# Experts begin after a first group of tiles has its queries; the other tiles' queries run between expert products; 64x64 blocks; a ring of 8 gather buffers

## The reference, cut to what matters

```
q      = h @ peer_wq                    # 1024 -> 2048: 8 heads x 2 halves x 128
s[j]   = q[j] @ keys[j % 2]             # 16 score rows of 128 keys per token
top16  = of each half; then top 16 of the 16 x 16 sums: expert numbers, gates
a      = gelu(h . u[expert])            # 8 heads x 16 = 128 experts per token
x     += g * sum(gate * a * v[expert])  # v, u: rows of 1024
```

## Time and profile before

| | us |
|---|---|
| median of 3 executions | 5278.08 (5275.77 to 5279.01) |
| the profiled execution | 5270.96 |
| its span, first to last instruction | 5269.2 |

### The profile page before, as it was taken

The page is one execution under the profiler, slowest core; times in us unless marked ns, Lnnn a source line. Parts: engine busy times, 40 slices in busy tenths (PEclk is TensorE's granted clock), DMA queues, the critical chain, the costliest instruction groups (busy, mean ns, idle before and its releaser), DMA issues.

```text
span 5269.2 us, 37538 instructions
## 1 busy us (share of the span) xinstructions
PE 4275.7 (81%) x11220; PEld 2065.7 (39%) x11220; DVE 3146.8 (60%) x8145; ACT 492.9 (9%) x1467; POOL 1498.5 (28%) x1376
## 2 busy tenths in 40 slices
PE   8999999987777777777777778999887777777777
PEld 1477635552323333232332225765442323233322
DVE  1052322348878788787886652523367878788665
ACT  1131110100000000000000001211100000000100
POOL 0000000004434444343444330000004444344443
PEclk9877698998898988988889997787798898988999
DMA  7100032349999999999999991011139999999998
GB/s 253 50 9 17 20 112 84 98 158 381 415 405 420 404 419 414 407 420 402 419 415 407 421 380 39 9 32 37 60 118 422 415 406 418 401 422 415 407 422 354
DMA packets 277772, 1489.70 MB, mean 283 GB/s; under 512 B 24152, under 2 KB 69848, under 8 KB 112704
## 3 DMA queue, kind: packets, MB, share of 16 engines
q0 software_dynamic: 185888, 1347.13, 62.1%
q1 hardware_dynamic: 66512, 114.85, 6.6%
q10 hardware_dynamic: 25168, 25.32, 1.4%
HBM read 1474.52 MB, written 12.68 MB: 282 GB/s over the span
## 4 chain that ended last, share of the span: by engine, by line
PE 44%; DMA 30%; DVE 13%; issue 10%; POOL 2%; ACT 1%; DVEq 0%; ACTq 0%; POOLq 0%; SPq 0%
DMA X<-in_uv_dram,hT 29%; PE ps L782 11%; PE ps L427 8%; PE ps L750 4%; PE ps L566 4%; PE ps L448 3%; PE ps L603 3%; POOL X L1518 2%; PE ps L578 2%; DVE hT L1407 1%; DVE X L1415 1%; PE ps L631 1%; DVE X L1349 1%; DVE X L1347 1%; DVE X L1350 1%
## 5 line engine op out<-in xcount | busy, mean ns | idle before, releaser
L782 PE MATMUL ps<-X,hT 128*128 128x512 f32 x5120 | 2468.0, 636 | 834.1 <-DVE hT L1407 833.1
L1518 POOL DMA_INDIRECT X<-in_uv_dram,hT x1280 | 1423.0, 1112 | 2387.6 <-PE ps L782 1628.4
L782 PEld LDWEIGHTS ps<-X,hT 128*128 128x128 f32 x5120 | 1007.1, 203 | 2294.5 <-issue 1239.9
L1415 DVE CUSTOM_DVE_ANT_0 X<-hT,X 128x1024 f32<-128x1024 f32 x1280 | 1541.6, 1224 | 608.8 <-DMA X<-in_uv_dram,hT 577.3
L1069 ACT ACTIVATE hT<-hT 128x2 f32<-128x2 f32 x640 | 130.1, 203 | 3068.2 <-DVE hT L1415 3068.1
L1407 DVE TENSOR_SCALAR hT<-ident,hT 128x128 f32<-128x128 f32 x1280 | 383.5, 344 | 1.5 <-ACT hT L1069 1.5
L427 PE MATMUL ps<-wring,hT 128*128 128x512 f32 (+2 forms) x736 | 308.4, 581 | 2.5 <-ACT yT L939 1.4
L750 PE MATMUL ps<-hT,wring 128*128 128x512 f32 x512 | 227.6, 598 | 2.2 <-ACT hT L860 2.2
L1488 POOL TENSOR_TENSOR X<-X 128x256 f32<-128x256 f32 x32 | 23.1, 724 | 702.4 <-DVE att L1202 692.6
L448 PE MATMUL ps<-wring,cT 128*2 128x512 f32 x384 | 181.7, 629 | 39.7 <-DMA wring<-in_ada_w_dram 19.1
L566 PE MATMUL ps<-X 64*128 64x256 f32 (+3 forms) x464 | 208.9, 597 | 3.7 <-ACT yT L939 1.4
(11 more groups left out here) (239 smaller groups left out, 2754.9 us busy)
## 6 DMA issues: line engine op xcount, KB each, us to landing
wring<-in_ada_w_dram SPq DMA_DIRECT2D x48, 1024.0 KB, 5.1
wring<-in_w_in_dram SPq DMA_DIRECT2D x24, 1024.0 KB, 5.2
X<-in_uv_dram,hT POOLq DMA_INDIRECT x1280
wring<-in_peer_wq_dram SPq DMA_DIRECT2D x16, 1024.0 KB, 5.6
wring<-in_w_out_dram SPq DMA_DIRECT2D x8, 1024.0 KB, 5.0
X<-scores SPq DMA_DIRECT2D x8, 1024.0 KB, 9.6
X<-mods ACTq DMA_DIRECT2D x12, 512.0 KB, 9.0
scores<-X ACTq DMA_DIRECT2D x16, 384.0 KB
```

What stands on the lines that cost most here:

```text
L782: m = pe.matmul(ps[:, h, :], dg[:, s % 8, :], uvr[:, s % UVRING, D + 512 * h:D + 512 * h + 512], start=(s == 0), stop=(s == SLOTS - 1))
L1415: m = v.tensor_tensor_reduce(uvr[:, s_ % UVRING, 0:D], xt, uvr[:, s_ % UVRING, 0:D], 1.0, 0.0, ALU.mult, ALU.add, adot[:, s_:s_ + 1])
L1518: g.indirect_dma_start(uvr[:, s % UVRING, :], None, a["uv"], bass.IndirectOffsetOnAxis(ap=istages[i % 2][:, s:s + 1], axis=0)).then_inc(S( ...
```

## The change

- **Groups.** `FIRST_GROUP = (CT, 1)`: layer 0's first group is the two context tiles, layer 1's its first tile; the rest is the other group (four and three tiles). Queries, scores and the choice of tile 0 are made for the first group alone; then experts begin. In the last tile of the first group (`with_rest`: tile 1 in layer 0, tile 0 in layer 1) TensorE runs the rest's queries between the expert products: 128 products of 512 (384) columns spread over 52 pairs, keys and scores two and five pairs after a query is done; VectorE picks the next tile's keys and pairs there straight from `stage`. `peer_wq` (8 MB) is loaded a second time in that tile, and the scores of the rest (bar its first tile) are stored there.
- **Indices** go out head by head: GpSimd may issue the first gathers after the first head.
- **64x64 blocks.** The diagonal is 64 columns wide (`ident2` holds two 64x64 identities one above the other). A slot's product is four products 64x64x512 instead of two 128x128x512; two slots make eight, ordered so that four different quarters of the array follow each other. The two halves of the tile's sum lie in four banks, and are added at the tile's end: ScalarE copies half of each to `xt` (2 activations), VectorE adds (2) and then multiplies.
- **`em` per pair**, not per slot; the diagonal ring has 16 places of 64 columns (before 8 of 128).
- **Ring of 8** gather buffers: `UVRING = 8`.
- **Modulation in column groups.** Each product has 32 stationary columns (two and thirty zeros), and four k-blocks go to the four 32-column groups of the array; a product with `pick` (2 columns) adds the four partial rows, another the bias. TensorE takes the halves one at a time. The last two chunks of layer 1 move from after the scores to between the norm transposes.

```diff
-MOD_BEFORE_FFN = ((7, 8), (9,), (), (), (), ())
+MOD_BEFORE_FFN = ((7, 8), (9,), (10,), (11,), (), ())
-UVRING = 11
+FIRST_GROUP = (CT, 1)
+REST_PAIRS = 52
+REST_GATES_AT = 59
+UVRING = 8
+DGRING = 16
+def query_done(j):
+    return next(q for q in range(REST_PAIRS) if KD * 2 * PH * (q + 1) // REST_PAIRS >= KD * (j + 1))
+def keys_at(j):
+    return query_done(j) + 2
+def scores_at(j):
+    return query_done(j) + 5
 # SyncE
-                for q in range(2):
-                    sp.wait_ge(S(f"sd{q}"), B(f"sd{q}", L) + 16 * PH)
-                for i in range(TILES - lo - 1):
-                    sp.wait_ge(S("istg"), B("istg", L) + 2 + PH * i)
-                    sp.dma_start(scn, scores_d[i + lo + 1]).then_inc(S("sl"), 16)
+                first, rest = groups(L)
+                load_scores(first, 1)
+                for c in range(4):
+                    send(L, a["peer_wq"][L], c * CH, "fq", 2 * PH + 4 * (c + 1), False)
+                load_scores(rest, 2 if len(first) > 1 else 1)
 # TensorE, modulation
-                        g = take(2)
-                        for k in range(KD):
-                            m = pe.matmul(ps[0:2, 6 + c % 2, :], cT[:, k, :], wsl(g, k, 0, CH), start=(k == 0), stop=False)
+                        for half in range(2):
+                            g = take(1)
+                            for j in range(GROUP_K):
+                                m = pe.matmul(ps[32 * j:32 * j + 32, 6 + c % 2, :], cT[:, half * GROUP_K + j, :], wring[:, g % WRING, j, :],
+                                              start=(half == 0), stop=(half == 1))
+                        if n_:
+                            gather_parts(chunks[n_ - 1])
 # TensorE, experts
-                    for s in range(SLOTS):
-                        pe.wait_ge(S("dg"), B("dg", L) + SLOTS * i + s + 1)
-                        for h in range(2):
-                            m = pe.matmul(ps[:, h, :], dg[:, s % 8, :], uvr[:, s % UVRING, D + 512 * h:D + 512 * h + 512],
-                                          start=(s == 0), stop=(s == SLOTS - 1))
+                    for q in range(SLOTS // BATCH):
+                        s = q * BATCH
+                        pe.wait_ge(S("dg"), B("dg", L) + SLOTS * i + s + 2)
+                        for h in range(2):
+                            v0 = uvr[:, s % UVRING, D + 512 * h:D + 512 * h + 512]
+                            v1 = uvr[:, (s + 1) % UVRING, D + 512 * h:D + 512 * h + 512]
+                            ends = dict(start=(s == 0), stop=(s == SLOTS - 2))
+                            pe.matmul(ps[0:HD, h, :], dg(slice(0, HD), s), v0[0:HD], **ends)
+                            pe.matmul(ps[HD:P, 2 + h, :], dg(slice(HD, P), s), v0[HD:P], **ends)
+                            pe.matmul(ps[HD:P, h, :], dg(slice(0, HD), s + 1), v1[0:HD], **ends)
+                            m = pe.matmul(ps[0:HD, 2 + h, :], dg(slice(HD, P), s + 1), v1[HD:P], **ends)
                         m.then_inc(S("em"), 1)
+                        if i == len(first) - 1:
+                            for j in range(2 * PH):
+                                if keys_at(j) == q:
+                                    key_scores(rest, 1, j)
+                            blocks = KD * 2 * PH
+                            for b in range(blocks * q // REST_PAIRS, min(blocks, blocks * (q + 1) // REST_PAIRS)):
+                                query(rest, 1, b // KD, b % KD)
 # ScalarE, end of a tile
+                    act.wait_ge(S("em"), B("em", L) + (SLOTS // BATCH) * (i + 1))
+                    nc.scalar.activation(x2[0:HD], ps[HD:P, 0:2, :], ACT.Copy)
+                    nc.scalar.activation(x2[HD:P], ps[0:HD, 2:4, :], ACT.Copy).then_inc(S("fold"), 1)
 # VectorE, end of a tile
-                    v.tensor_tensor(gj, ps[:, 0:2, :], gtab[:, s, :].rearrange("p (a b) -> p a b", b=512), ALU.mult).then_inc(S("xa"), 1)
+                    v.tensor_tensor(gj[0:HD], ps[0:HD, 0:2, :], x2[0:HD], ALU.add)
+                    link(v.tensor_tensor(gj[HD:P], ps[HD:P, 2:4, :], x2[HD:P], ALU.add))
+                    v.tensor_tensor(g4, g4, gtabs[s], ALU.mult).then_inc(S("xa"), 1)
 # GpSimd
-                            g.wait_ge(S("em"), B("em", L) + SLOTS * i + used + 1)
+                            g.wait_ge(S("em"), B("em", L) + SLOTS // BATCH * i + (used + SLOTS) // BATCH - SLOTS // BATCH + 1)
```

More of the change, by code:

```diff
@@ L180, in slot_uses, with groups @@
     return (SLOTS - 1 - r) // UVRING + 1
+def groups(layer):
+    tiles = list(range((0, CT)[layer], TILES))
+    return tiles[:FIRST_GROUP[layer]], tiles[FIRST_GROUP[layer]:]
+def query_done(j):
[4 more added lines that the diff above has]
+    return query_done(j) + 5
 def att_base(kind, layer):
@@ L776, in _, with query @@
-                pe.wait_ge(S("fse"), B("fse", L) + 2 * PH)
+                first, rest = groups(L)
+                wq = [None]
+                def query(group, n_, j, k):
+                    c0, N = group[0] * P, len(group) * P
+                    if k == 0:
+                        if j % 2 == 0:
+                            wq[0] = take(1)
+                        if n_ or j >= 2:
+                            pe.wait_ge(S("fqe"), B("fqe", L) + 2 * PH * n_ + j - 1)
+                    m = pe.matmul(ps[:, 4 + j % 2, 0:N], by_columns(wq[0])[:, k, j % 2 * P:(j % 2 + 1) * P], hT[:, k, c0:c0 + N],
+                                  start=(k == 0), stop=(k == KD - 1))
+                    if k == KD - 1:
+                        m.then_inc(S("fq"), 1)
@@ L812, in modulation, with row_out @@
                 def modulation(M, chunks, end):
-                    for c in chunks:
+                    def row_out(c):
                         act.wait_ge(S("mps"), B("mps", M) + c + 1)
@@ L1385, in _, with indices, scores_in @@
-                link(v.tensor_copy(top, top_1))
-                indices_out(idxn_1, early)
-                v.wait_ge(S("istg"), B("istg", L) + 2)
-                gates_ahead(0)
+                first, rest = groups(L)
+                def indices(i, h):
+                    last = choose_pairs(top, istages[i % 2][:, h * TOPK:(h + 1) * TOPK], h)
+                    last.then_inc(S("istg"), 1)
+                    v.wait_ge(S("istg"), B("istg", L) + PH * i + h + 1)
+                def scores_in(group, n_, j):
+                    N = len(group) * P
+                    v.wait_ge(S("fs"), B("fs", L) + 2 * PH * n_ + j + 1)
+                    if len(group) > 1 and (j >= 2 or n_ and len(first) > 1):
+                        stored = n_ if len(first) > 1 else 0
+                        v.wait_ge(S(f"sd{j % 2}"), B(f"sd{j % 2}", L) + 16 * (PH * stored + j // 2))
+                    v.tensor_copy(stage[:, j % 2, 0:N], ps[:, 6 + j % 2, 0:N]).then_inc(S("fse"), 1)
@@ L1389, in _, with staged @@
+                def staged(w):
+                    return stage[:, w, 0:P]
                 if L < LAST:
```

294 lines of the change are left out of this document (153 added, 141 removed).

## The result

| | before | after |
|---|---|---|
| median, us | 5277.6 (5275.77 to 5279.01) | 5562.48 (5558.89 to 5572.1, 4 runs) |
| ratio, 95% interval | | 1.0543 (1.0525 to 1.0561) |
| span of the profiled execution | 5269.2 | 5563.4 |
| mean granted clock | 0.884 | 0.761 |

The change makes the kernel slower by 285 us. The forecast was slower by 81: the right side, under a third of the size. First the windows of the changed kernel, stage by stage (length, busy us of PE, PE's loads, DVE, ACT, POOL, then granted clock, DMA share, GB/s). The rows are: the start; the last output projection up to layer 0's first dot; layer 0's experts; layer 1's heads, its queries, its experts.

A forecast was written before the change was run, and what follows sets the result against it. DMA bounds the experts (share 0.99 to 1.00). Terms +229 + 45 + 13 - 35 - 18 - 113 - 40 = +81 on 5271 give 5352; with the median 7 us above, 5360 us, range 5150 to 5600.

The forecast's parts named there:

- Ring (A): Gathers around each `choose_pairs`: eight buffers leave the DMA queue dry, 4.0 us for 48 blocks, 2.3 for 16: +229 us.
- the added bytes (B): Experts: `peer_wq` loaded again and score stores moved inside, two loads fewer: +45 us, ends 0 and 61.
- Pairs without a choice: Expert pairs with no `choose_pairs`: loop of 18.2 us, 19.9 at half clock, against 20 for four pairs; holds, barely.
- Tile ends (C): From one tile's last dots to the next: queue some 6 us dry, 10 at half clock; net +13 us.
- Four quarters: TensorE's expert products: four 64x64 quarters run side by side, so a pair takes 1.7 us at full clock.
- second and third rivals: Expert products: quarters run two at a time (5650 us, chance 0.10) or one at a time (some 6450, 0.03).
- Start (D): Start of the kernel: DMA then bounds, first norm over at 101 instead of 136.7 us; -35 us.
- Layer 1's chunks (E): Seven chunks on TensorE's path before the second norm: from 9.0 to 6.4 us each; -18 us.
- Layer 0's queries (F): Queries before layer 0's experts: first group only, VectorE bounds at 11.3 us per head; -113 us.
- layer 1's (G): Queries before layer 1's experts, 144.5 us before the change: -40 us (-30 to -48).
- the first ("no gap opens"): Experts: time from a pair's release to its transfer is shorter than taken, A is 0; 5170 us, chance 0.23.
- The fourth: Rival: start and queries bring nothing, as DMA and the choice bound them already; 5560 us, chance 0.04.

The follow-up runs named there:

- a_warm: The changed kernel with four unused products more after each pair's, in the tiles without queries, to keep TensorE busy: 5539.91 us, 1.0504.
- b_ring8_pair: The kernel before with a ring of 8 and its buffers freed by pairs instead of by slots, 128x128 blocks kept: 5936.46 us, 1.1254.
- a_early: The changed kernel with VectorE's diagonals of the previous pair ahead of a pair's dots, and a pair's own ahead of its `choose_pairs`: 5246.38 us, 0.9946.
- a_early_mix: The changed kernel with diagonals moved ahead of dots and choices, plus a ninth gather buffer in tiles behind the one with queries: 5203.12 us, 0.9862.

## Why the forecast was wrong, step by step

- **Ring (A)**: right in its mechanism: issue at T + 16.1 for 16.0, interval 35.3 for 34.3, DMA share 0.90 to 0.93 in choice tiles (forecast the same). Mis-sized: with the share of the added bytes (B) the blocks cost 202 + 82 and, for the eighth block of a tile, an estimated 8 x 4 = 32 of what follows it: 316 us against 229 + 45. The miss is 42, and 34 of it lie in the six tiles without queries: a block costs 4.8 us there instead of 4.0 (202 and an estimated 24, forecast 192). In the two with queries the forecast had 37 for A and 45 for B, 82 together, and the seven intervals measure just 82; how that divides between ring and bytes no run shows.
- **Pairs without a choice**: "It holds, barely" is the step that failed. It had no term in the sum, and costs 68 us in the two plain tiles and 24 behind the last block, the largest miss. I took issue to second dot at 8.8 us from a dry queue. In a full tile, with a DMA share of 0.95, it is 11.1 us. The issue comes 11.3 us after the last dot at a mean clock of 0.68 (forecast 9.4 at full and 11.1 at half), and still 10.1 in a_warm at 0.96. So four pairs take 22.4 us, not 18.2 to 19.9. A margin of 0.1 us at the low clock should have been a term with bounds. More than half of the loss is the clock (a_warm gives back 20 of 35 us in the last tile and 21 of 27 in layer 0's). The signal per pair costs such pairs 47 us a tile with 128x128 blocks (b_ring8_pair); with 64x64 blocks its part was not measured. The forecast's own signs say the same: 325 us for a plain tile, 313 without the 12 of its end, measured 343 and 350; 355 to 365 for a tile with a choice, measured 374 to 389.
- **Tile ends (C)**: 23 at the ends and 48 in the pairs behind them, 71 against 13. The dry time was forecast (6 to 10, measured 8.6); what was wrong is the gain set against it, that buffers now fit the tile's 128 slots, which gave back little, and the shorter products at the end, which ran in part at the low clock.
- **Four quarters**: right, 1.9 us per pair at full clock. ("The fourth case below falls away" can only mean the second and third rivals.)
- **Start (D)** -21 for -35: the DMA share went from 0.76 to 0.85 only, so the transfers do not come back to back. **Layer 1's chunks (E)** +2 for -18. No experiment was made on either. **Layer 0's queries (F)** -123 for -113, **layer 1's (G)** -46 for -40: right.
- **Rivals**: the first ("no gap opens") had the DMA share against it and is out for this kernel; a_early shows what it takes to make it nearly true: the issue at T + 6.5. (The 40 us that it adds back in its 5170 are derived from nothing.) The fourth is out by the 184 us ahead of the experts; that it named 5560 us, nearly the time measured, is chance. The range up to 5600 holds the result because it was stretched over rivals that did not come true.

Of the difference, 192 us beyond the forecast in the experts are these terms (42 + 92 + 58), and 22 more are missing ahead of them. That ring, signal and order carry the loss is shown by runs; the split of it over the parts of a tile is read from the traces. Why a_early_mix's choice tiles with nine buffers still stand at 330 to 345 us where the intervals are back at 30.5 was not tested further.

## What to carry to other kernels

Where an engine both consumes buffers and computes what frees them, put the freeing work ahead of its long blocks: here that order was worth 316 us in the changed kernel and 295 in the kernel before with eight buffers, and 12 with eleven. A smaller ring must be checked by the whole loop, from the last read to the landing under load, for every kind of stretch, and a margin of a few tenths of a us is a cost to put into the sum. A signal for two buffers at once can cost more than a buffer: with a ring of eight and 128x128 blocks it took 289 us, the buffer from nine to eight 112.

## What the hardware showed beyond the expected

- Four 64x64 blocks of f32 products run fully side by side: 16 instructions of 512 columns in 1.9 us at full clock.
- With TensorE busy half of the time, the granted clock changes between 1.00 and 0.50 from pair to pair in the same tile (0.68 and 0.72 over whole tiles); with 128x128 blocks and the same ring it was 0.89 and 0.97. Three windows of the last tile:

```profile
5299.00:5302.00 3.00, 1.95 (x16) 0.51 (x16) 1.76 (x6) 0.20 (x1) 2.55 (x2) 1.00 0.57 164
5304.00:5307.00 3.00, 2.47 (x16) 0.51 (x16) 0.47 (x4) 0.20 (x1) 0.86 (x1) 0.79 0.97 339
5311.00:5314.00 3.00, 2.38 (x12) 0.80 (x16) 1.80 (x6) 0.20 (x1) 0.94 (x1) 0.50 0.99 418
```

- One buffer fewer costs very different amounts: 129 us in the mean of the two from eleven to nine, 112 from nine to eight, and 595 from eight to seven where the signal comes by pairs.
